# Value projection of the dilated attention pairs: plain token order in the projection, rows brought into residue order by SBUF-to-SBUF transfers

## The reference, cut to what matters

```python
ATT_GROUPS = ((128, 1), (512, 4), (2048, 16))      # window, dilation
...
def dilated_group(q, k, v, slopes, window, dilation):
    # query t attends to t, t-d, ..., t-window: keys gathered by residue class mod d
    t.reshape(B, L, dilation, H, E).transpose(0, 2, 1, 3, 4)
    ...
    o = jnp.einsum('bdnhqk,bdnkhe->bdnqhe', p / s, vw)
```

## Time and profile before

| what | value |
|---|---|
| runs | 1059.77 us median of 3 (1059.34 to 1061.94) |
| span of the profiled execution | 1062.9 us, 3.1 us above the median of the runs |
| TensorE busy, weight loads busy | 1000.6 us (94%), 865.7 us (81%) |
| VectorE, ScalarE, POOL busy | 500.0, 367.9, 404.2 us (47%, 35%, 38%) |
| mean granted TensorE clock | 0.978 of 2.4 GHz |
| moved by DMA | 111.36 MB, 105 GB/s |

### The profile page before, as it was taken

The page is one execution under the profiler, slowest core; times in us unless marked ns, Lnnn a source line. Parts: engine busy times, 40 slices in busy tenths (PEclk is TensorE's granted clock), DMA queues, the critical chain, the costliest instruction groups (busy, mean ns, idle before and its releaser), DMA issues.

```text
span 1062.9 us, 12769 instructions
## 1 busy us (share of the span) xinstructions
PE 1000.6 (94%) x5071; PEld 865.7 (81%) x5071; DVE 500.0 (47%) x720; ACT 367.9 (35%) x499; POOL 404.2 (38%) x163
## 2 busy tenths in 40 slices
PE   2699999999999999999999989799999999999995
PEld 2579989979989798987778879688888888888884
DVE  5945486773333756597845367732232223200006
ACT  6433324241232212144422233443453435421213
POOL 4668331313121223223423424435344443444354
PEclk9989999999999999999999999899999999999998
DMA  9623221212041545535222332212323223232312
GB/s 323 195 80 119 80 80 40 80 41 80 1 158 40 165 153 189 168 100 178 80 80 80 127 131 82 93 65 79 118 79 100 97 94 103 79 119 83 116 40 80
DMA packets 94819, 111.36 MB, mean 105 GB/s; under 512 B 1930, under 2 KB 88118, under 8 KB 94774
## 3 DMA queue, kind: packets, MB, share of 16 engines
q1 hardware_dynamic: 94774, 110.72, 31.7%
HBM read 108.62 MB, written 2.10 MB: 104 GB/s over the span
## 4 chain that ended last, share of the span: by engine, by line
PE 59%; issue 22%; DVE 11%; POOL 5%; ACT 2%; DMA 1%; SPq 0%; POOLq 0%; ACTq 0%; DVEq 0%
PE bank L925 58%; POOL w_lo L582 4%; DVE part L1269 1%; DVE ada L1269 1%; DVE x L1661 1%; DVE m_lo L1583 1%; DMA x_in<-in_x_dram 1%; DVE h_lo L1286 1%; DVE sgb L1581 1%; DVE inv L1493 0%; DVE gelu L1660 0%; DVE part L1280 0%; ACT m_hi L855 0%; DVE part L1271 0%; DVE sgb L1579 0%
## 5 line engine op out<-in xcount | busy, mean ns | idle before, releaser
L582 POOL TENSOR_TENSOR w_lo<-w_raw,w_hi 128x2048 fp32r<-128x2048 f32 x73 | 337.0, 4616 | 602.7 <-ACT w_hi L650 602.7
L925 PE MATMUL bank<-h_hi,w_hi 128*128 128x512 f32 x768 | 307.1, 400 | 6.2 <-DVE h_lo L1286 6.2
L925 PE MATMUL bank<-h_lo,w_hi 128*128 128x512 f32 x768 | 304.1, 396 | 0.0
L925 PE MATMUL bank<-h_hi,w_lo 128*128 128x512 f32 x768 | 303.8, 396 | 0.0
L650 ACT ACTIVATE w_hi<-w_raw 128x2048 fp32r<-128x2048 f32 x73 | 139.4, 1909 | 274.6 <-PE bank L925 235.2
L925 PEld LDWEIGHTS bank<-h_hi,w_hi 128*128 128x128 f32 x768 | 147.8, 192 | 38.5 <-issue 8.1
L925 PEld LDWEIGHTS bank<-h_hi,w_lo 128*128 128x128 f32 x768 | 147.3, 192 | 31.6
L925 PEld LDWEIGHTS bank<-h_lo,w_hi 128*128 128x128 f32 x768 | 147.6, 192 | 30.3
L925 PE MATMUL bank<-w_hi,h_hi 128*128 128x256 f32 x256 | 87.9, 343 | 3.6 <-POOL w_lo L582 2.1
L925 PE MATMUL bank<-w_lo,h_hi 128*128 128x256 f32 x256 | 87.2, 341 | 0.0
L925 PE MATMUL bank<-w_hi,h_lo 128*128 128x256 f32 x256 | 87.1, 340 | 0.0
(11 more groups left out here) (243 smaller groups left out, 1382.3 us busy)
## 6 DMA issues: line engine op xcount, KB each, us to landing
w_raw<-in_w_in_dram SPq DMA_DIRECT2D x32, 1024.0 KB, 5.2
ada<-in_w_ada_dram SPq DMA_DIRECT2D x24, 1024.0 KB, 6.7
w_raw<-in_w_up_dram SPq DMA_DIRECT2D x22, 1024.0 KB, 5.1
w_raw<-in_w_down_dram SPq DMA_DIRECT2D x11, 1024.0 KB, 4.9
w_raw<-in_w_out_dram SPq DMA_DIRECT2D x4, 1024.0 KB, 6.9
x_in<-in_x_dram SPq DMA_DIRECT2D x4, 512.0 KB, 7.1
w_raw<-in_w_in_dram SPq DMA_DIRECT2D x8, 256.0 KB, 8.5
w_raw<-in_w_branch_a_dram SPq DMA_DIRECT2D x2, 1024.0 KB, 4.9
```

Source lines behind the costliest of these rows:

```text
L582: pool.tensor_tensor(wlo[slot][:, :], raw[slot][:, :], whi[slot][:, :].bitcast(F32), ALU.subtract).then_inc(lo_done, 1)
L925: return pe.matmul(o, lhsT, rhs, start=start, stop=stop, **kw)
```

## The change

The projection of dilated value units takes the tokens in plain order. VectorE copies the four tiles into a new buffer `va_tok` (4 x 256 floats for each of 128 partitions), and SP brings the rows into residue order with 16 transfers for each dilated pair, SBUF to SBUF: for each tile t and each class r, the 32 rows r, r+4, ... of tile t go to rows 32t to 32t+31 of `va[:, r, :]`, 1 KB for each row. They are put in SP's loop ahead of the load of unit s+4. SP waits for `O` of the pair before and for VectorE's copies. TensorE waits for the transfers (`va_in`) before `O(p)`, and VectorE waits for the transfers of the dilated pair before, when it writes `va_tok` again, in place of its wait for `O` of the pair before.

```diff
+FIRST_DILATED = next(p for p in range(PAIRS) if pair(p)[2] > 1)
+MOVES = TT * pair(FIRST_DILATED)[2]
...
+        va_tok = at("va_tok", 114, [P, TT, 256])
...
+        va_in = sem("va_in")
...
@@ sync: SP's queue
+            def values_by_residue(p):
+
+                s, d = U_PAIR + 3 * p + 2, pair(p)[2]
+                ready(sp, ("O", p - 1, 1))
+                for t in range(TT):
+                    evacuated(sp, ("g", s, t))
+                for t in range(TT):
+                    rows_ = slice(t * P // d, (t + 1) * P // d)
+                    for r in range(d):
+                        sp.dma_start(va[rows_, r, :], va_tok[r:P:d, t, :]).then_inc(va_in, 16)
+
             for u in range(U_UP):
...
+                for p in range(PAIRS):
+                    if pair(p)[2] > 1 and u == U_PAIR + 3 * p + 2 + 4:
+                        values_by_residue(p)
                 if u >= 3:
                     load_unit(u, unit_source(u), u % 2)
@@ tensor: products
-            def dilated_tokens(t, d):
-
-                if d == 1:
-                    return plain_tokens(t)
-                return lambda a: a.rearrange("p (l res) -> p res l", res=d)[:, t, :]
-
...
-                        d = 1 if u < U_PAIR else pair((u - U_PAIR) // 3)[2]
-                        ins = token_tile(b[:, 0:256], parts, hT, dilated_tokens(t, d))
+                        ins = token_tile(b[:, 0:256], parts, hT, plain_tokens(t))
@@ tensor: small products, O(p)
+                        if pair(p)[2] > 1:
+                            pe.wait_ge(va_in, 16 * MOVES * (p - FIRST_DILATED + 1))
@@ vector: copies of a value unit
-                        if p:
+                        if d == 1 and p:
                             ready(dve, ("O", p - 1, 1))
+                        elif d > 1 and p > FIRST_DILATED:
+                            dve.wait_ge(va_in, 16 * MOVES * (p - FIRST_DILATED))
                         for t in range(TT):
                             b = ready(dve, ("g", u, t))
-                            release(dve.tensor_copy(va[:, t, :], b[:, 0:256]), ("g", u, t))
+                            release(dve.tensor_copy((va if d == 1 else va_tok)[:, t, :], b[:, 0:256]), ("g", u, t))
```

## The result

The change makes the kernel slower by 0.9%: 1069.11 us median of four runs (1067.41 to 1070.61) against 1060.86 us (1059.34 to 1062.99), ratio 1.0086, 95% interval 1.0063 to 1.011. The forecast was 1046.5 us in a range of 1040 to 1063. (It stood on the first three runs of before, whose median was 1059.77; four give 1060.86.) The profiled run took 1067.41 us with a span of 1065.7; the profiled execution of before had a longer span than its runs' median lets expect, so the two spans differ by 2.8 us only, and sizes of whole kernels are taken from the medians.

What follows compares the result with a forecast made beforehand. TensorE's ordered work, paced in dilated units by strided weight loads, was taken to bound the kernel: -45.2 (plain tokens) + 16.4 (late pairs) + 8.0 (VectorE) + 7.5 (clock) = -13.3 us, giving 1046.5 us, range 1040 to 1063.

Steps and rivals of the forecast that it cites:

- the three late pairs: Pairs 3, 4, 5: SP issues moves only after VectorE's sums, so O waits; 4.3, 4.6 and 7.5 us lost, 16.4 together.
- an issue costs more: Rival, SP's queue: 48 us per us of issue price over three late pairs; 1055.6 us at 0.53; chance 0.28.
- Plain tokens, -45.2 us: TensorE, value units 14, 17, 20, 23: each falls from 22.7 to 11.4 us, saving 11.3 us each.
- The price of an issue, 0.34 us: SP's queue: each small transfer takes 0.34 us to issue, ends 0.29 and 0.53; a set holds SP 5.4 us.
- over 0.62 us an issue: Sign on SP that the forecast is wrong; from 0.62 us per issue the change was to bring no gain.
- Landing, 2.1 us: Transfers land 2.1 us after issue, so all 16 have landed 7.2 us after the first issue.
- Pair 2 is hidden, 7.3 us to spare: Before O(2): transfers landed at 309.8 us, wanted at 317.1, so no loss.
- Behind the moves the weights of units 18, 21, 24 and 27 start 5.4 us later: SP's weight loads behind the moves: delay hidden beside other work; without that cover at most 5.4 us each.
- VectorE's lateness, 8.0 us: TensorE waits at the fourth tile for VectorE's value copies, 4.0 us in each of units 20 and 23.
- The clock, 7.5 us: TensorE at half clock after waits: 2.5 us each after fourth tiles of units 20 and 23 and after pair 5.
- hidden everywhere: Rival: moves never delay O; only 8.0 us and 2 x 2.5 us of clock remain, 1028 us; chance 0.10.
- paid one after another: Rival: each transfer takes 2.1 us alone, a set 33.6 us; +98 us, 1145 us; chance 0.04.
- plain order saves nothing: Rival, dilated value units: no gain, 16.4 us and 2.5 us of clock are loss; 1079 us; chance 0.03.

Runs made afterwards that it cites:

- The probe: Kernel before plus unread test transfers in SP's wait in slot 17: five forms, SBUF-to-SBUF or from HBM, 8, 32 or 128 rows; 1060.22 us beside 1060.21.
- The cure: The change with transfers earlier in SP's queue, plus VectorE copying value tile 0 between the two partial sums in slots 20 and 23: 1019.3 us, ratio 0.9611.

## Why the prediction was wrong

The forecast failed at the price of an issue, which I had at 0.34 us and which is 0.63 us. The mechanism of the three late pairs was named rightly, and so was the rival, "an issue costs more", at 0.28. But it isn't that rival's arithmetic that gives the result: at 0.63 it makes 0.29 x 48 = 13.9 us and a kernel as fast as before, and "slower" was to need 0.68. The measured loss has two more parts, pair 2 and the clock. That the sign agrees with a rival of mine is partly luck. Step by step:

- *Plain tokens, -45.2 us.* Right, by the loads of 0.119 us. Net of what VectorE takes back, the run with the plain order alone shows -34 us.
- *The price of an issue, 0.34 us.* This step failed first, and the sign that I had named for it, over 0.62 us an issue, came. The probe tells two reasons apart. I had taken the price from two issues at the kernel's start, and behind the first of a row from HBM they lie 0.46 us apart; and they read from HBM, where SBUF-to-SBUF starts lie 0.63 us apart. That is above my upper end of 0.53 too, which I had misread: the earlier trace rows show a 1 MB load of 0.60 us, and by it the sum would have been -0.8 us. The three waits came to 31.6 us in place of 7.4 + 4.6 + 7.5 = 19.5: 12 us.
- *Landing, 2.1 us.* Right (2.2).
- *Pair 2 is hidden, 7.3 us to spare.* Its transfers were; what failed is "Behind the moves the weights of units 18, 21, 24 and 27 start 5.4 us later. That lies beside other work". I asked when TensorE wants unit 18, and not who stands in ScalarE's order behind the high part of unit 18: the `ss` banks, and by them O(2). This loss, too, comes from the price: with SP held for 5.0 us (half the transfers) the wait isn't there, with 7.2 us (two large ones) it is 1.8 us, with 10.4 us it is 4.3. Moving this one set cures 6.6 us, of which 4.3 are the wait; behind it the granted clock was 0.50 for 5 us.
- *VectorE's lateness, 8.0 us.* Right in place, too large. Where the transfers are early it is 4.0 us in unit 23, as forecast, but 1.1 in unit 20: I had called slot 20 alike, while in the kernel before its products start at 373.15 us, 2.1 us behind VectorE's first copy at 371.1, since they wait for POOL. In the change it is 3.7 us of waiting in all; there the late O and its half clock also gave VectorE time. The cure brings 7.7 us (1026.95 to 1019.3), so some clock with it.
- *The clock, 7.5 us.* Too small. By the timeline, O(3), O(4) and O(5) took 3.75 us each in place of 1.95 (5.4 us), the modulation products behind them 1.9 us more in all, unit 20 took 16.9 us, of which 2.1 were a wait, and unit 23 15.4 with 1.6 of waiting, 3.3 and 2.4 us over 11.5; 0.5 us in unit 26. That is 13.5 us, 6 more than forecast. I had taken the half clock after pairs 3 and 4 as covered by VectorE; but it slowed O as well, ahead of that cover. That a dilated unit hardly feels it, as I had said, the run with the transfers alone shows: its products lie 0.24 us apart at a granted clock of 0.55 and 0.233 at full.

Together 12 + 6.6 + 6 - 4.3 = 20 us, of 21.6 between -13.3 and the +8.3 of the medians. This adds waits of single executions to a difference of medians, so it is good to about 2 us, and the rest, 1.3 us, says nothing. In the forecast's own range two sums are off by 0.4 us: they are -23.2 and -4.6 us, which moves its ends by less than a microsecond and decides nothing.

The rule of the Trainium skill that smaller transfers are mostly overhead (DMA: Bandwidth & Descriptors, Rules for kernel authors) points the right way for SP's time; but the run with two large ones gained only 7.7 us, about what pair 2 was worth, since two landings in a row took the place of the issues.

The rivals: "hidden everywhere" is what the same transfers do at another place in the queue; "paid one after another" is out by 2.2 us landings behind starts 0.63 us apart; "plain order saves nothing" is out by the run with the plain order alone.

Left open: why an issue with SBUF at both ends is dearer than one that reads HBM; why the first of a row is cheaper in most forms (not with 8 rows, where it took 0.74 us); and how long the granted clock stays at half. In the change that was 8.0 us of work behind 10.5 us of idleness, 9.2 behind 8.9, 5.3 behind 12.2 and 5 behind 4.3, in no order of the idle times, so the forecast's single row of 6.1 us could not give it.

## What to carry to other kernels

Where a queue works in order, the place of new transfers decides more than their number: put them where the queue stands waiting for something later than the data they need, and not behind that wait. Here that turned 8 us of loss into 33 us of gain with the same 64 transfers. Price a transfer from a row of the same kind: both ends, and not the first of its row. And when a load is pushed back, look at the engine that takes it and at all that stands behind it in that engine's order, not only at the load's last user.

## What the runs showed of the hardware that was not expected

- A weight load of 128x128 whose 128 columns lie four floats apart takes 0.33 us and paces matmuls at 0.236 us; with neighbouring columns it is 0.19 and 0.119 us.
- SP's issue costs about 0.6 us for SBUF to SBUF, whether 8, 32 or 128 rows of 1 KB, and 0.42 us from HBM; starts 0.63 and 0.46 us apart. The first of a late set took 0.47 us, the first from HBM 0.345.
- After 10.4 us without work TensorE had 0.50 of its clock for 8.0 us of work, after 12.2 us for 5.3. Behind a wait of only 2.1 us in unit 20 it ran 0.9 us at full clock and then 3.5 us at 0.51. O's 16 small matmuls took 3.75 us in place of 1.95.
